# A decoder layer in split fp32: a subtraction one product later, part loads ahead of a store, and rest parts taken from SBUF in the second pass

## The reference, cut to what matters

```python
def ffn_sublayer(x, w_up, w_down, g_pre, g_post):
    h = rmsnorm(x, g_pre)
    a = jnp.square(jax.nn.relu(jnp.einsum('ntd,df->ntf', h, w_up)))
    return x + rmsnorm(jnp.einsum('ntf,fd->ntd', a, w_down), g_post)
```

## Time and profile before

| | us |
|---|---|
| median of 3 runs | 2098.05 (2096.04 to 2098.82) |
| profiled execution, its own time | 2096.81 |
| its span | 2095.1 |
| busy: PE, DVE, ACT, POOL | 1983.6, 1346.6, 1227.2, 890.7 |

### The profile page before, as it was taken

One profiled execution on the slowest core, in us unless ns is written; L12 is line 12 of the kernel. 1 busy time (PEld: TensorE's weight loads), 2 busy tenths in 40 slices (PEclk: granted clock), 3 DMA queues, 4 the chain that ended last, 5 costly groups with the idle time before them and its releaser, 6 DMA issues.

```text
span 2095.1 us, 39222 instructions
## 1 busy us (share of the span) xinstructions
PE 1983.6 (95%) x15342; PEld 1946.1 (93%) x15342; DVE 1346.6 (64%) x1958; ACT 1227.2 (59%) x1790; POOL 890.7 (43%) x646
## 2 busy tenths in 40 slices
PE   7999999999965999999999999989999999999995
PEld 6999989999945999999999999989999999999994
DVE  3455643522258777777777777766666666666666
ACT  5233421422234677777777777767777777777782
POOL 0000022211170666565665656544444444444574
PEclk9999998999956999999999999999999999999996
DMA  5421121342221555656556565695656556556532
GB/s 171 158 71 51 52 81 61 113 138 85 87 85 43 168 181 186 203 172 194 179 187 201 174 194 177 191 351 184 205 184 205 184 184 207 185 186 208 187 104 86
DMA packets 270767, 328.16 MB, mean 157 GB/s; under 512 B 8128, under 2 KB 236872, under 8 KB 268975
## 3 DMA queue, kind: packets, MB, share of 16 engines
q1 hardware_dynamic: 267104, 315.66, 46.4%
q10 hardware_dynamic: 3479, 9.99, 1.3%
HBM read 253.79 MB, written 74.22 MB: 157 GB/s over the span
## 4 chain that ended last, share of the span: by engine, by line
PE 69%; DVE 17%; POOL 6%; issue 3%; ACT 3%; DMA 2%; SPq 0%; DVEq 0%; POOLq 0%; ACTq 0%
PE banks L1610 21%; PE banks L1965 14%; PE banks L1967 14%; PE banks L1966 14%; DVE mlp_sums L1464 4%; DVE quads L1459 4%; DVE splits L1430 3%; ACT banks L1009 1%; DVE mlp_sums L1457 1%; PE banks L1755 1%; ACT mlp_hi L1023 1%; POOL mlp_sums L754 1%; POOL mlp_sums L749 1%; POOL sq_sum L696 1%; DMA mlp_parts<-mlp_kept 1%
## 5 line engine op out<-in xcount | busy, mean ns | idle before, releaser
L1965 PE MATMUL banks<-h_part,splits 128*128 128x272 f32 x1792 | 525.5, 293 | 37.3 <-DVE quads L1447 21.3
L1965 PE MATMUL banks<-mlp_parts,splits 128*128 128x272 f32 x1792 | 517.5, 289 | 8.4 <-DVE splits L1430 5.6
L1967 PE MATMUL banks<-h_part,splits 128*128 128x272 f32 x1792 | 522.2, 291 | 0.0
L1966 PE MATMUL banks<-h_part,splits 128*128 128x272 f32 x1792 | 519.9, 290 | 0.0
L1967 PE MATMUL banks<-mlp_parts,splits 128*128 128x272 f32 x1792 | 517.0, 288 | 0.0
L1966 PE MATMUL banks<-mlp_parts,splits 128*128 128x272 f32 x1792 | 516.1, 288 | 0.0
L1965 PEld LDWEIGHTS banks<-h_part,splits 128*128 128x128 f32 x1792 | 341.1, 190 | 44.3 <-issue 36.2
L1965 PEld LDWEIGHTS banks<-mlp_parts,splits 128*128 128x128 f32 x1792 | 336.6, 188 | 9.7 <-ACT splits L1014 7.9
L1966 PEld LDWEIGHTS banks<-h_part,splits 128*128 128x128 f32 x1792 | 341.6, 191 | 0.0
L1967 PEld LDWEIGHTS banks<-h_part,splits 128*128 128x128 f32 x1792 | 341.0, 190 | 0.0
L1966 PEld LDWEIGHTS banks<-mlp_parts,splits 128*128 128x128 f32 x1792 | 340.8, 190 | 0.0
(11 more groups left out here) (234 smaller groups left out, 3439.5 us busy)
## 6 DMA issues: line engine op xcount, KB each, us to landing
raw_up<-in_w_up SPq DMA_DIRECT2D x128, 512.0 KB, 7.7
raw_down<-in_w_down SPq DMA_DIRECT2D x128, 512.0 KB, 4.5
mlp_parts<-mlp_kept SPq DMA_DIRECT2D x56, 1088.0 KB, 8.2
mlp_kept<-mlp_hi SPq DMA_DIRECT2D x32, 952.0 KB, 4.5
mlp_kept<-mlp_sums SPq DMA_DIRECT2D x32, 952.0 KB, 5.7
w_raw<-in_w_in SPq DMA_DIRECT2D x40, 512.0 KB, 3.6
w_raw<-in_w_out SPq DMA_DIRECT2D x32, 512.0 KB, 3.4
x_kept<-x1T SPq DMA_DIRECT2D x4, 1088.0 KB, 4.0
```

The source lines that it names most:

```text
L1965: nc.tensor.matmul(out, wh, xh, start=first, stop=False, skip_group_check=not STARTS[i])
L1966: nc.tensor.matmul(out, wh, xl, start=False, stop=False, skip_group_check=not STARTS[i])
L1967: ins = nc.tensor.matmul(out, wl, xh, start=False, stop=j == pairs - 1, skip_group_check=not STARTS[i])
```

## The change

Four edits.
1. `mlp_low` of the group before stands after take 3 of a group, where it stood after take 2.
2. At the step between the passes SP issues the first two loads of parts ahead of `store_hi(30)`, and the other five ahead of `store_lo(30)`.
3. In the second pass ACT no longer copies to PSUM; it rounds to `splits` alone.
4. In the second pass DVE's low part waits for that (`part_hi`) and reads both the weights and the rounded value from SBUF.

```diff
         def high_of(N):
-            if N < N_UP:
-                return flat(4 + 2 * (N % 2), 1024).rearrange("p (j c) -> p j c", c=P)
-            return banks[:, 4 + (N - N_UP) % 4, :].rearrange("p (j c) -> p j c", c=P)
+            return flat(4 + 2 * (N % 2), 1024).rearrange("p (j c) -> p j c", c=P)
...
         def high_free(N):
-            if N < N_UP:
-                return N - 1 if N >= 2 else 0
-            d = N - N_UP
-            return N_UP + d - 3 if d >= 4 else N_UP - 1 + d // 2
+            return N - 1 if N >= 2 else 0
...
             for g in range(UP_GROUPS):
-                if g > 0:
+                if 0 < g < UP_GROUPS - 1:
                     store_hi(g - 1)
                     store_lo(g - 1)
...
             for i in range(NP):
+                if i == 2:
+                    store_hi(UP_GROUPS - 2)
                 sp.wait_ge(product_done, N_UP - NP + i // 2 + 1)
                 load_part(0, i)
+            store_lo(UP_GROUPS - 2)
             sp.wait_ge(product_done, N_UP)
...
             def high_copy(N):
 
                 source_ready(N)
+                if N >= N_UP:
+                    return
                 if high_free(N):
...
             def low_part(N):
 
-                dve.wait_ge(hi_copied, N + 1)
+                if N < N_UP:
+                    dve.wait_ge(hi_copied, N + 1)
                 if split_free(N):
                     dve.wait_ge(product_done, split_free(N))
-                nc.vector.tensor_tensor(split_of(N, 1), weight_of(N), high_of(N), ALU.subtract).then_inc(part_lo, 1)
+                if N >= N_UP:
+                    dve.wait_ge(part_hi, N + 1)
+                high = high_of(N) if N < N_UP else split_of(N, 0).bitcast(F32)
+                nc.vector.tensor_tensor(split_of(N, 1), weight_of(N), high, ALU.subtract).then_inc(part_lo, 1)
...
-                if i == 2 and G > 0:
+                if i == 3 and G > 0:
                     mlp_low(G - 1)
```

## The result

The changed kernel took 2134.35 us (median of 4 runs, 2132.90 to 2135.42), the kernel before 2097.05 beside it: ratio 1.0179, 95% interval 1.0163 to 1.0195. It is slower, as forecast, but by 37 us where 9 were forecast, and outside the range. The profiled span grew from 2095.1 to 2133.5 us, by 38.4.

What follows compares the result with a forecast made beforehand. PE was taken to bound the second pass, with gains only in the first pass or the step between; -18.0 + 5.6 + 12.5 + 9.0 = +9.1 us took the median of 2098.05 to 2107, own range 2101 to 2114, wider 2093 to 2117.

Steps and rivals of the forecast that it cites:

- Step 1: First pass: moving mlp_low behind take 3 removes PE's stall of 0.62 us in 29 groups, -18.0 us.
- Step 2: Between the passes: no product waits for parts, but squares 31 wait for store_lo behind all seven loads, +5.6 us.
- Step 3: Second pass: low parts with two SBUF operands are blocked by GpSimd, +12.5 us in 57 groups, +9.0 in the last chunk.
- the term of +12.5: Second pass, 57 groups: four blocked low parts make DVE's group 10.77 us where PE wants 10.55, +12.5 us.
- that of +9.0: Last chunk: GpSimd's two added squares block more low parts, 12.35 us a group for five groups, +9.0 us.
- The port costs little: Rival, second pass: low parts win each race and GpSimd waits, only the last chunk pays; 2086 to 2095 us, 14%.
- the store lands early: Rival, between the passes: stores don't queue behind loads, so -9.5 instead of +5.6 us there; 2092 us, 6%.
- The port costs more: Rival, second pass: a free low part also meets GpSimd or blocks come 0.05 later; 11.0 a group, 2121 us, 10%.
- Steps 2 and 3 about half as dear: Rival, between the passes and in the second pass: about half the forecast costs there; 2098 us, no change, 12%.

Runs made afterwards that it cites:

- The run with nothing read by GpSimd: Changed kernel, with GpSimd's four block sums of the second pass replaced by a constant memset: 2082.62 us, ratio 0.9941 to the kernel before.
- edit 2 alone: Kernel before, with only the new SP order at the step (loads of first parts ahead of group 30's stores): 2099.06 us, ratio 1.0017.
- the wait alone: Kernel before, with the second pass's low part also waiting for part_hi but still reading ACT's copy in PSUM: 2095.43 us, ratio 0.9994.
- the SBUF operand alone: Kernel before, with ACT's early second-pass copy put in SBUF, both low-part operands read there, no wait for part_hi: 2120.15 us, ratio 1.0113.
- both +45.8: Kernel before, with ACT's PSUM copy dropped in the second pass, low part waiting for part_hi and reading both operands from SBUF: 2143.63 us, ratio 1.0220.
- the fastest kernel: Kernel before, with mlp_low behind take 3 and group 30's two stores between the fourth and fifth part loads: 2072.32 us, ratio 0.9891.

## Why the prediction was right in its direction and wrong in its size

**Step 1 was right.** -18.0 forecast; -18.0 between the marks, -17.1 as a run of its own, where the step takes back 1.9. `mlp_low` takes its undisturbed time there, 2.13 where the earlier trace rows has 2.81, as the working said:

```profile
1000.87 2.13 DVE L1468 TENSOR_TENSOR mlp_sums<-mlp_sums,mlp_hi 128x1904 f32<-128x1904 f32 x1
```

**Step 2 had the right mechanism and came out 2.5 us short.** SP, DVE and PE at the step in the changed kernel:

```profile
1344.30 2.74 SPq L531 DMA_DIRECT2D mlp_kept<-mlp_sums  x1
```
```profile
1359.36 1.01 DVE L1461 SCALAR_TENSOR_TENSOR mlp_sums<-quads 128x816 f32<-128x816 f32 x1 [11.91 <-DMA mlp_kept<-mlp_sums]
```
```profile
1361.33 0.56 PE L1969 MATMUL banks<-mlp_parts,splits 128*128 128x272 f32 x1 [11.35 <-DVE y_sum L1451]
...
1372.54 0.36 PE L1969 MATMUL banks<-mlp_parts,splits 128*128 128x272 f32 x1 [2.28 <-DVE y_sum L1454]
...
1374.22 0.43 PE L1969 MATMUL banks<-mlp_parts,splits 128*128 128x272 f32 x1
1374.45 0.43 PE L1970 MATMUL banks<-mlp_parts,splits 128*128 128x272 f32 x1
```

The store behind all seven loads holds squares 31. They were forecast for 1375.8 on the old scale, which is 1358.3 on the new (18.0 earlier in the first pass, 0.5 later at its start); they came at 1359.36, 1.1 later. The working had put about 1 us for the store to be reported, for which it had no row; from its issue to its landing the store took 15.0:

```profile
mlp_kept<-mlp_sums SPq DMA_DIRECT2D x1, 952.0 KB, 15.0
```

From there to take 231 the working had 16.3 us, and it took 17.8. Up to take 228 it was right within 0.1: that take came 12.5 after the squares, in the working and in the trace. The rest lies behind it. PE resumes at 1372.54, and from 1374 on 14 matmuls are 0.227 apart instead of 0.125, at a low granted clock, which is 1.4 us. The run with nothing read by GpSimd has the same order at the step. There no low part is blocked, PE's second pause is 1.25 us instead of 2.28, and the matmuls behind it stay 0.125 apart:

```profile
1368.13 0.36 PE L1975 MATMUL banks<-mlp_parts,splits 128*128 128x272 f32 x1 [1.25 <-DVE y_sum L1460]
...
1369.71 0.29 PE L1975 MATMUL banks<-mlp_parts,splits 128*128 128x272 f32 x1
1369.84 0.29 PE L1976 MATMUL banks<-mlp_parts,splits 128*128 128x272 f32 x1
```

From squares 31 to take 231 it takes 15.44, 2.4 less than the changed kernel: 1.0 is the blocked low part, which the working had, and 1.4 the matmuls, which it had not: it kept the clock of before, 1.00. No run changed the clock by itself. The other way round, GpSimd's second and third sum of squares 31 take 1.23 us beside DVE's low parts from SBUF, and 0.78 and 0.77 with edit 2 alone.

**Step 3 failed at one sentence:** "Each low part now waits for `part_hi` ... and ends 1.4 us after it, where PE needs it after three more products, 4.5 us: also nothing by itself." By itself it is nothing, and the run with the wait alone shows so. The blocks by themselves cost what was forecast, and the run with the SBUF operand alone shows so: 10.78 against 10.77. The sum took each at its own price and added. But a pace is a loop, and together the two make another loop, which is longer. In the kernel with blocks alone, DVE goes from low part 5 through 6, 0 and 1 to low part 2 in 0.95 + 1.98 + 0.95 and a take's 0.27, 4.15 us. With the wait, low part 2 needs what stands in the loop above between the end of low part 5 (1717.49) and its own start (1722.07): a take, PE's two products and ACT's rounding, 4.58. The difference is 0.43 a group, and 10.77 + 0.43 = 11.20. The reserve of 4.5 us was spent: the three blocked low parts behind low part 2 took 5.94. Of the second pass's error of 26.7 us, 57 x 0.43 = 24.5 is this; the other 2 are the last chunk's, six groups of 12.41 instead of five of 12.35. So the term of +12.5 measured 37, and that of +9.0 measured 11.2.

So the three runs read: wait 0, operand +22.3, both +45.8. The parts don't add, and only the pair shows what the change costs. The pair also leaves out ACT's copy, which the other two keep; no run has the wait and the SBUF operand with the copy kept, and none gave `splits` a slot more to open the loop.

**The rivals.** "The port costs little" and "the store lands early" fell: GpSimd won each time, four in a group, three of them by 0.12 to 0.21 us from its start to the start of the low part's record; and the store held DVE for 11.9 us. "The port costs more" gave 11.0 a group and 2121 and was nearest; but its reason, blocks 0.05 longer or a fifth block, isn't what happened. "Steps 2 and 3 about half as dear" fell as well, and its sum was off: half of 27.1 us beside the -18.0 is 4.5 us faster, 2093.6, and not 2098. The rule of the Trainium skill, SBUF — State Buffer, section Who interferes with whom, on two SBUF inputs held for the duration of each block. The 58 and 120 fixed cycles of the Trainium skill, VectorE: DVE Perf Modes, section on the TRN2 errata, don't show as a difference: 677 ns at best with one operand in PSUM, 675 with both in SBUF.

**What was to show it.** Most of it came: 21.19 a group in the first pass, DVE idle for a DMA at squares 31, low parts of 0.68 and near 1.7, 12.4 at the end. Two things differed and point at the loop. PE is busy for 96% there, not for 98%, and it waits for the take (L1454) and not for the low part (L1434). And DVE has 26 of 400 us idle, nearly all of it in waits for ACT's rounding (its waits from 1500 to 1900):

```profile
DVE splits L1434 <- ACT splits L1014: 25.4, 71, 0.6
```

That is two waits in each group. The one ahead of low part 3 costs nothing, for that low part is blocked anyway; the one ahead of low part 2 lies in the loop. With the SBUF operand alone DVE has no wait for ACT in that stretch.

## What to carry to other kernels

When a change adds both a wait and a longer duration, don't price them one by one: follow the loop through all engines back to its own instruction in the next group, and take the longest loop, with the longer durations in it. A buffer that is freed by the consumer (here a slot of `splits`, by a product) closes such a loop. An early copy in another memory can look like waste on an idle engine's account, and be what keeps two engines from blocking each other and a producer off the critical loop.

Of a change in three parts, measure each alone: here the best kernel has the first, another form of the second and not the third, 2072.3 us against 2134.4.

## What the runs showed of the hardware beside that

PE's pause of 11.35 us at the step was followed by a granted clock of 0.50, from 1.00 ahead of it, and after the pause of 2.28 us soon behind it the clock was low again, 0.53 (columns as in the earlier trace rows):

```profile
1361.30:1367.20 5.90, 5.87 (x26) 5.90 (x27) 2.43 (x4) 2.31 (x2) 5.82 (x6) 0.50 0.02 4
...
1374.20:1377.60 3.40, 3.40 (x17) 3.40 (x17) 1.55 (x3) 0.99 (x2) 2.30 (x2) 0.53 0.98 247
```

Matmuls are 0.227 apart in both, which is the lower of its two levels, 1.2 GHz, where 0.125 goes with 2.4. The first stretch cost nothing here: the low part of product 230 waits for ACT, which stands behind GpSimd's sums of squares 31, and take 227 follows it with no wait for PE. The second cost the 1.4 us. With edit 2 alone, after a pause of 10.8 us, the granted clock was 0.90 over the next 19.5 and a second pause, of 1.5 us, was followed by none of the slow matmuls. At the step of the fastest kernel, PE was busy for 12.51 of 16 us in shorter pieces and the granted clock stayed at 1.00. So what a low clock costs depends on whether PE's products are what the next step waits for.
